# Keys of the second attention layer turned on VectorE, biases added on VectorE, sample products spread over three steps

## The reference, cut to what matters

```python
q, k, v = proj[..., :D], proj[..., D:2*D], proj[..., 2*D:3*D]
lf = log_sigmoid(proj[..., 3*D:] + b_f)
c = cumsum(lf, axis=1)                      # samples: over 256 cached and 16 new rows
s = einsum('bqhd,bkhd->bhqk', q, k) * 64 ** -0.5
s = s + cq[:, :, :, None] - ck[:, :, None, :]
s = where(kpos <= qpos, s, -inf)
o = einsum('bhqk,bkhd->bqhd', softmax(s), v)
y = o @ w_out
```

## Time and profile before

| | |
|---|---|
| median of 3 runs | 1886.15 us (1883.71 to 1886.22) |
| profiled execution, span | 1885.1 us (the page gives no time of its own beside the span) |
| TensorE busy | 1849.9 us (98%) |
| VectorE busy | 983.0 us (52%) |
| ScalarE busy | 722.0 us (38%) |
| GpSimd busy | 225.9 us (12%) |
| DMA | 259.38 MB, mean 138 GB/s |
| granted TensorE clock, mean | 0.997 |

### The profile page before, as it was taken

How to read it: one execution, slowest core, us unless ns; L and a number is a source line. 1 busy time by engine, 2 the same in 40 slices (tenths; PEclk the granted TensorE clock), 3 DMA queues, 4 the chain that set the end, 5 groups by cost and what they waited for, 6 DMA issues and landing times.

```text
span 1885.1 us, 29064 instructions
## 1 busy us (share of the span) xinstructions
PE 1849.9 (98%) x12004; PEld 1642.4 (87%) x12004; DVE 983.0 (52%) x1569; ACT 722.0 (38%) x1144; POOL 225.9 (12%) x357
## 2 busy tenths in 40 slices
PE   8999999999999999999999999999999999999998
PEld 8777799998888887799998899998897777999986
DVE  4557653443567778743443664443465576543434
ACT  4246443333255454333332343333242463433321
POOL 3114070000011222230000100000031230000000
PEclk9999999999999999999999999999999999999999
DMA  7357254433353433444433434433364562444332
GB/s 246 128 203 229 81 160 123 129 129 123 117 164 105 125 116 104 118 139 125 124 134 123 146 101 125 132 124 125 110 206 150 200 221 90 137 132 124 128 129 79
DMA packets 179171, 259.38 MB, mean 138 GB/s; under 512 B 14717, under 2 KB 122349, under 8 KB 179040
## 3 DMA queue, kind: packets, MB, share of 16 engines
q1 hardware_dynamic: 161184, 197.18, 32.3%
q0 software_dynamic: 17856, 60.35, 9.9%
HBM read 243.19 MB, written 13.19 MB: 136 GB/s over the span
## 4 chain that ended last, share of the span: by engine, by line
PE 90%; DVE 4%; ACT 3%; issue 1%; DMA 1%; SPq 0%; DVEq 0%; ACTq 0%
PE ps L1605 14%; PE ps L1607 14%; PE ps L1606 14%; PE ps L1617 11%; PE ps L1615 11%; PE ps L1616 11%; PE ps L1833 1%; PE ps L1951 1%; PE ps L1938 1%; PE ps L1638 1%; PE ps L1888 1%; PE ps L1671 1%; DVE w_lo L785 1%; PE ps L1908 1%; PE ps L1673 1%
## 5 line engine op out<-in xcount | busy, mean ns | idle before, releaser
L785 DVE TENSOR_TENSOR w_lo<-w_raw,w_hi 128x1024 fp32r<-128x1024 f32 x370 | 452.1, 1228 | 709.1 <-ACT w_hi L439 707.9
L439 ACT ACTIVATE w_hi<-w_raw 128x1024 fp32r<-128x1024 f32 x370 | 389.3, 1059 | 803.5 <-DMA w_raw<-in_w_ffn_in_dram 363.1
L1605 PE MATMUL ps<-xT_hi,w_hi 128*128 128x384 f32 x1568 | 528.4, 337 | 2.5 <-issue 1.4
L1607 PE MATMUL ps<-xT_hi,w_lo 128*128 128x384 f32 x1568 | 527.0, 336 | 0.0
L1606 PE MATMUL ps<-xT_lo,w_hi 128*128 128x384 f32 x1568 | 526.9, 336 | 0.0
L1605 PEld LDWEIGHTS ps<-xT_hi,w_hi 128*128 128x128 f32 x1568 | 294.8, 188 | 5.2 <-issue 5.1
L1606 PEld LDWEIGHTS ps<-xT_lo,w_hi 128*128 128x128 f32 x1568 | 294.8, 188 | 0.1
L1607 PEld LDWEIGHTS ps<-xT_hi,w_lo 128*128 128x128 f32 x1568 | 294.8, 188 | 0.0
L1617 PE MATMUL ps<-w_hi,hT_lo 128*128 128x512 f32 x528 | 210.6, 399 | 0.0
L1616 PE MATMUL ps<-w_lo,hT_hi 128*128 128x512 f32 x528 | 208.1, 394 | 0.0
L1615 PE MATMUL ps<-w_hi,hT_hi 128*128 128x512 f32 x528 | 207.4, 393 | 0.0
(11 more groups left out here) (329 smaller groups left out, 2021.8 us busy)
## 6 DMA issues: line engine op xcount, KB each, us to landing
w_raw<-in_w_ffn_in_dram SPq DMA_DIRECT2D x352, 256.0 KB, 3.2
w_raw<-in_w_ffn_out_dram SPq DMA_DIRECT2D x176, 256.0 KB, 2.9
w_raw<-in_w_fox_in_dram SPq DMA_DIRECT2D x96, 256.0 KB, 2.9
k_c<-in_cache_fox_k_dram POOLq DMA_DIRECT2D x32, 512.0 KB, 5.3
v_c<-in_cache_fox_v_dram POOLq DMA_DIRECT2D x32, 512.0 KB, 4.0
w_raw<-in_w_hgrn_in_dram SPq DMA_DIRECT2D x64, 256.0 KB, 2.9
w_raw<-in_w_fox_out_dram SPq DMA_DIRECT2D x32, 256.0 KB, 2.9
out_dram<-kv_tok POOLq DMA_DIRECT2D x4, 1024.0 KB, 5.0
```

The lines of the kernel that those rows point to most:

```text
L439: nc.scalar.activation(w_hi[:, slot, :], w_raw[:, slot, :], ACT.Copy).then_inc(hi_ready, 1)
L785: V.tensor_tensor(w_lo[:, slot, :], w_raw[:, slot, :], w_hi[:, slot, :].bitcast(F32), ALU.subtract).then_inc(lo_ready, 1)
L1605: mm(out, w_hi[:, slot, cols], x_hi[:, k, :], start=k == 0, stop=False, skip_group_check=True)
L1607: last = mm(out, w_lo[:, slot, cols], x_hi[:, k, :], start=False, stop=k == KD - 1, skip_group_check=True)
```

## The change

1. Biases and masks of the scores leave TensorE. SyncE writes the running sums to DRAM (`sums_p`, `sums_s`) and reads them back as broadcasts over partitions (`bias_p` for two prompt heads, `bias_s` for one sample), two buffers each, one broadcast after each step, each issued after the one before has landed (`next_bias`). GpSimd adds the mask in place (`mask_prompt_bias`, `mask_sample_bias`). Queries are scaled by -1/8, the sums keep their sign, and VectorE's tensor_tensor_reduce adds bias to scores, writes the sum to SBUF and takes its minimum; exp then reads SBUF with scale -1. The splits, selectors and the mask copies for TensorE go.
2. In layer 3 (`AHEAD`) cached keys are not turned in the loop. In the feed-forward of layer 2 GpSimd loads them in eight parts (`k_nat`), VectorE transposes them in blocks of 32x32 (8 instructions a part), GpSimd stores them to DRAM as `keys_t`, and SyncE loads them in layer 3, turned, in three buffers. GpSimd copies the new keys beside them.
3. In layer 3 the sample products of one step are spread over three (`steps_apart`): scores of n, transposes of n-1, s_out of n-2, fold of n-3. In layer 0 the order within a step changes: s_fold stands between other products, and s_keys is halved around s_turn.

```diff
+            def first_biases(i, j):
+                f = FOX[i]
+                sync.wait_ge(*at(f["c"], 1 + DB))
+                sync.dma_start(sums_p[j, :, 0:P], cp[:, 0:P]).then_inc(f["bias_in"][0], 16)
+                sync.dma_start(sums_p[j, :, P:T], cp[:, :]).then_inc(f["bias_in"][0], 16)
+                for hf in range(2):
+                    sync.dma_start(sums_s[j, :, :, hf, :], craw[8 * hf:8 * hf + 8, :, :]).then_inc(f["bias_in"][0], 16)
+                sync.wait_ge(*at(f["bias_in"], LOADED))
+                for k in range(2):
+                    prompt_bias_in(i, j, k)
+                for b in range(2):
+                    sample_bias_in(i, j, b)
+            def prompt_bias_in(i, j, k):
+                sync.dma_start(bias_p[:, k % 2, :, :], sums_p[j, 2 * k:2 * k + 2, :].partition_broadcast(P)).then_inc(
+                    FOX[i]["bias_in"][0], 16)
+            def sample_bias_in(i, j, b):
+                sync.dma_start(bias_s[:, b % 2, :, :],
+                               sums_s[j, :, b, :, :].rearrange("h f k -> h (f k)").unsqueeze(1).broadcast_to(
+                                   [HEADS // 2, DT, 2 * (PAST + DT)])).then_inc(FOX[i]["bias_in"][0], 16)
+            def next_bias(i, j, t):
+                f = FOX[i]
+                sync.wait_ge(*at(f["bias_in"], LOADED + 16 * (3 + t)))
+                if t % 2:
+                    sync.wait_ge(*at(f["nmax"], t + 1))
+                    prompt_bias_in(i, j, t // 2 + 2)
+                else:
+                    sync.wait_ge(*at(f["s_nmax"], t))
+                    sample_bias_in(i, j, t // 2 + 1)
+            def turned_keys(i, first, end):
+                ...
+                    else:
+                        sync.wait_ge(*at(f["s_scores"], n - KV + 1))
+                    sync.dma_start(k_t[:, n % KV, :, 0:PAST], keys_t[b, hf * WCOLS:(hf + 1) * WCOLS, :].rearrange(
+                        "(g p) k -> p g k", p=P)).then_inc(KEYS[f"in{n % KV}"][0], 16)
...
-                    chunks(w_fox_in[j], s["mix"], 6, 0 if i else 1)
-                    chunks(w_fox_out[j], s["out"], 2)
+                    if i == AHEAD:
+                        chunks(w_fox_in[j], s["mix"], 6, 0, 5 * CU)
+                        turned_keys(i, 0, KV)
+                        chunks(w_fox_in[j], s["mix"], 6, 5 * CU)
+                    else:
+                        chunks(w_fox_in[j], s["mix"], 6, 1)
+                    first_biases(i, j)
+                    chunks(w_fox_out[j], s["out"], 2, 0, RING)
+                    for t in range(1, 2 * DB - 2):
+                        if i == AHEAD:
+                            turned_keys(i, t + KV - 1, t + KV)
+                        if t < 2 * DB - 3:
+                            next_bias(i, j, t)
+                    chunks(w_fox_out[j], s["out"], 2, RING)
...
+            def turn_keys_ahead(n):                        # VectorE, in the feed-forward of layer 2, chunks 1 to 8
+                dve.wait_ge(*at(KEYS["loaded"], 16 * (n + 1)))
+                if n:
+                    dve.wait_ge(*at(KEYS["stored"], 64 * n))
+                for a in range(TWIN):
+                    ins = V.transpose(k_turn[:, :, :, a], k_nat[:, a, :])
+                ins.then_inc(KEYS["turned"][0], 1)
...
-                        V.tensor_reduce(nmx[:, (n - 1) % 2, 2:3], ps[:, SS_BANK, 0:PAST + DT], AX_X, ALU.max,
-                                        negate=True).then_inc(f["s_nmax"][0], 1)
+                        if n % 2:
+                            dve.wait_ge(*at(f["bias"], sample_bias(n // 2)))
+                        V.tensor_tensor_reduce(out=p_s[:, (n - 1) % 2, :], in0=ps[:, SS_BANK, 0:PAST + DT],
+                                               in1=bias_s[:, (n - 1) // 2 % 2, (n - 1) % 2, :], scale=1.0, scalar=LARGEST, op0=ALU.add,
+                                               op1=ALU.min, accum_out=nmx[:, (n - 1) % 2, 2:3]).then_inc(f["s_nmax"][0], 1)
...
+                        if n % 2 == 0:
+                            dve.wait_ge(*at(f["bias"], prompt_bias(n // 2)))
+                        for q, lo, hi in ((0, 0, P), (1, P, T)):
+                            ins = V.tensor_tensor_reduce(out=p_p[:, n % 2, lo:hi], in0=ps[:, bank, lo:hi],
+                                                         in1=bias_p[:, n // 2 % 2, n % 2, lo:hi], scale=1.0, scalar=LARGEST, op0=ALU.add,
+                                                         op1=ALU.min, accum_out=nmx[:, n % 2, q:q + 1])
...
+                def mask_prompt_bias(k):                   # GpSimd
+                    blocks = bias_p[:, k % 2, :, :].rearrange("p e (t c) -> p e t c", t=NTOK)[:, :, 0:NTOK:2, :]
+                    G.tensor_tensor(blocks, blocks, causal[:, :].unsqueeze(1).unsqueeze(1).broadcast_to([P, 2, 2, P]),
+                                    ALU.subtract).then_inc(f["bias"][0], 1)
+                def mask_sample_bias(b):
+                    new = bias_s[:, b % 2, :, PAST:]
+                    G.tensor_tensor(new, new, new_mask[:, :].unsqueeze(1).broadcast_to([P, 2, DT]), ALU.subtract).then_inc(
+                        f["bias"][0], 1)
...
                 for n in range(KV, 2 * DB + KV):
-                    if n < 2 * DB:
+                    if n < 2 * DB and i == AHEAD:
+                        pool.wait_ge(*at(f["s_scores"], n - KV + 1))
+                        new_keys(n)
+                    elif n < 2 * DB:
                         pool.wait_ge(*at(f["ktr"], n - KV + 1))
                         load_k(n)
+                    if i == AHEAD and 2 <= n - KV < 2 * DB - 2:
+                        next_mask(n - KV)
                     pool.wait_ge(*at(f["s_o"], n - KV + 1))
                     if n < 2 * DB:
                         load_v(n)
                     if n - KV + 2 < 2 * DB:
                         load_new(n - KV + 2)
+                    if i != AHEAD and 2 <= n - KV < 2 * DB - 2:
+                        next_mask(n - KV)
...
-                        mm(out, sel_p[:, h:h + 1].broadcast_to([CROWS, P]), c_p[:, :], start=True, stop=False, skip_group_check=True)
-                        mm(out.rearrange("p (t c) -> p t c", t=NTOK)[:, 0:NTOK:2, :], ident_r[:, :],
-                           causal_r[:, :].rearrange("p (t c) -> p t c", t=NTOK)[:, 0:NTOK:2, :], start=False, stop=False,
-                           skip_group_check=True)
...
-                    mm(ps[:, SS_BANK, 0:PAST + DT], sel_s[:, n % 2, :], c_s[:, n // 2, :], start=False, stop=True,
-                       skip_group_check=True).then_inc(f["s_scores"][0], 1)
...
+                def steps_apart():                         # layer 3; layer 0 keeps a loop like the one before
+                    for n in range(HEADS):
+                        if n >= 3 and n % 2:
+                            p_out((n - 3) // 2)
+                        if n % 2 == 0:
+                            p_scores(n // 2)
+                        ...
+                        if n >= 2:
+                            s_out(n - 2)
+                        if n:
+                            s_turn(n - 1)
+                            p_turn(n - 1)
+                        s_pairs(n)
+                    s_fold(HEADS - 3)
+                    out_piece(0, 0)
+                    s_turn(HEADS - 1)
+                    p_turn(HEADS - 1)
+                    out_piece(0, 1)
+                    s_out(HEADS - 2)
+                    p_out(KD - 1)
+                    out_piece(1, 0)
+                    s_fold(HEADS - 2)
+                    s_out(HEADS - 1)
+                    out_piece(1, 1)
+                    s_fold(HEADS - 1)
```

377 lines of the change are left out of this document (226 added, 151 removed).

## The result

The changed kernel takes 1924.29 us (median of 4 runs, 1918.36 to 1928.68) against 1885.05 us of the kernel before on the same chip: a ratio of 1.0207, 95% interval 1.0191 to 1.0223. It is slower by some 39 us. The forecast was 1876, the range ended at 1892.

The account below looks back on a forecast made before the run. TensorE, busy 98% of the span, was taken as the bound, with DMA deciding in L3's changed loop. L0 -4.2, L3 -6.8 and +1.0 ahead of the loops gave -10.0: 1885.1 to 1875.1, forecast 1876 us, range 1858 to 1892.

Parts of the forecast that it names:

- Removed products: Attention loops: bias, causal and key-transpose products leave TensorE, 9.9 us in L0 and 23.8 in L3, if TensorE stayed the limit.
- Added DMA: Attention loops: broadcasts and other transfers need 63.4 us of fully used DMA in L0, 64.0 in L3; loops 72.7 and 73.4.
- rival B: Loops: SyncE issues each bias only after the last landed, so a landing bounds the step; about +13, 1899 us; chance 0.13.
- DMA allows a gain of 5.3 and 4.6: DMA's limit on the two attention loops against 78.0 us: 5.3 us less in L0, 4.6 less in L3.
- Added waits in L0: L0's loop: VectorE and TensorE wait for late GpSimd masks, leaving L0 a gain of 4.2 us.
- rival D: L0's loop: GpSimd's mask and VectorE's scaling of probabilities exclude each other in SBUF; +4 to +8 us, 1882; chance 0.05.
- New operation on VectorE: Head loops: tensor_tensor_reduce takes as long as the reduce it replaces, nothing added; exp from SBUF within 0.1 us.
- Ahead of the loops: Before both loops: output weights land some 4 us later behind the biases; 0.5 us a layer, +1.0 in all.
- Keys in the third feed-forward: Third feed-forward: 64 VectorE transposes, up to 0.67 us each, and added DMA are covered; nothing, bounds 0 to 2 us.

Follow-up runs that it names:

- e4: Changed kernel without the broadcasts inside the loops and their masks, first biases added again, computation partly left out: 1887.83 us, ratio 1.0010.
- e3: Changed kernel with prompt and sample bias broadcasts counted on two semaphores, so two can be under way: 1913.75 us, ratio 1.0146.
- e10: Changed kernel without broadcasts inside the loops, but with all GpSimd masks, laid again on the first biases: 1896.27 us, ratio 1.0056.
- e8: Kernel before plus only turned keys and spread sample products, with the new order inside a step; biases stay on TensorE: 1886.66 us, ratio 1.0010.
- e5: The changed kernel run again unaltered, as the measure for runs beside it: 1923.74 us, ratio 1.0206.
- e15: Keys' part alone, biases on TensorE, order inside a step as before, turning blocks behind chunks 1 to 8: 1877.85 us, ratio 0.9961.
- e12: Keys' part alone, biases on TensorE, order as before, turning blocks behind chunks 1, 2, 4, 5, 7, 8, 9, 10: 1875.19 us, ratio 0.9953.
- e2: Changed kernel with layer 3's keys again transposed by TensorE in its loop, so only the biases' part, new order in both loops: 1915.85 us, ratio 1.0155.

## Why the prediction was wrong

**Removed products: right in the main.** With no broadcasts and masks (e4) loop 0 is 4.9 us shorter and loop 3 13.0; without what the new order costs (below) it would be 8.6 and 18.7, beside 9.9 and 23.8 of removed products. After its waits the text had booked 4.2 and 6.8.

**Added DMA: the step that failed.** The bytes and rates were right: the DMA engines' busy time in the loops is 0.76 x 85.8 = 65.2 us and 0.77 x 84.2 = 64.9, forecast 63.4 and 64.0. Wrong was the next line, a share of 0.95 outside 6 unused us, from which a shorter loop followed. Measured: a share of 0.88 and 0.89 over the 72.5 and 71.0 us in which transfers run, and 13 us around them with almost none, so 72.5 + 13.3 in place of 66.7 + 6 in loop 0. And as the engines fill, everything lands later, which the text has only under its rival B. The loads of v, in the first loop before, the two loops of the changed kernel, and the second of e3:

```profile
v_c<-in_cache_fox_v_dram POOLq DMA_DIRECT2D x13, 512.0 KB, 4.0
v_c<-in_cache_fox_v_dram POOLq DMA_DIRECT2D x13, 512.0 KB, 5.5
v_c<-in_cache_fox_v_dram POOLq DMA_DIRECT2D x13, 512.0 KB, 6.7
v_c<-in_cache_fox_v_dram POOLq DMA_DIRECT2D x13, 512.0 KB, 7.2
```

A high share alone does not hold TensorE. In the second loop of e4, without broadcasts, the DMA engines have 0.96 over 40 us and TensorE works through:

```profile
1505.00:1545.00 40.00, 38.39 (x518) 23.33 (x516) 26.20 (x135) 26.27 (x102) 15.29 (x31) 1.00 0.96 320
```

That the three buffers per operand and the waits across queues keep the changed loops from using the engines so well is argued; no run has more buffers. The Trainium skill, "DMA: Bandwidth & Descriptors", section "Where 436 GB/s comes from", has some 358 GB/s for one core. Over 40 us the runs stay below it, 298 in e3 (share 0.98) and 320 in e4; over the ten us from 4 to 14 of the changed kernel they move 388, so it is no bound for a short stretch. The forecast of "DMA allows a gain of 5.3 and 4.6" should have been a loss: +6.2 and +4.7 measured.

**Rival B: named, only a part.** Its cadence came true: from the third on, the broadcasts inside the loops go out 5.3 and 5.2 us apart (156.8 to 204.1 and 1534.5 to 1581.0), where it decides from 5.2 on. But by its own sum that gives only about 1887 (79.4 and 75.2 us against 76.2 each, less 2.2, plus 1), and even 5.7 gives 1899. (The range was said to take in B up to 5.5; by the same sum 5.5 is 1894, outside it.) With the chain gone (e3) the loops keep most of their loss: of 11 to 13 us it explains 3.5 to 4.8 by the stages. The medians give it up to 11 of the 39. It got 0.13.

**Added waits in L0: right in kind, a little small, and with another reason in it.** Masks alone cost 7.5 us in e10; the text had 9.9 less 4.2, 5.7. It had them as waits for a late mask, and VectorE does wait 7.8 us for sample masks in e10. Beside that stands the lock of rival D, which had a chance of 0.05: the scalings take 9.2 us longer. How the 7.5 us divide is not shown; D's price of 4 to 8 us on top of the 5.7 was too high, its mechanism is real.

**A step that is missing: the order.** The text costed what was removed and never the fold moved into the middle of the score and value products, or the keys' transposes cut in two. Under the limit of TensorE that is 3.6 us in loop 0 and 5.7 in loop 3.

**New operation on VectorE: right.** The sum with minimum takes 442 ns for 128x272 (e4), as long as the reduction it replaces (0.44 in the earlier trace rows), and 0.08 us for reading the accumulator. ScalarE's exp of these takes 522 ns from SBUF (e4) against 487 from PSUM (before), within the 0.1 us allowed.

**Ahead of the loops: mis-sized.** +0.5 each became +5.5 and +8.0. The text had a landing some 4 us later and took little of it to reach TensorE. SyncE issued 3.9 and 6.5 us later, the first square then shared the engines with 1.34 MB of broadcasts and landed 6.7 us after its issue (2.8 before), and the copies of turned keys stood behind it in ScalarE's queue. Waits in the changed kernel between 100 and 136 us, and ScalarE's in e8 (100 to 128):

```profile
ACT w_hi L527 <- DMA w_raw<-in_w_fox_out_dram: 15.6, 2, 9.9
PE ps L1991 <- ACT kT L664: 5.7, 1, 5.7
...
ACT w_hi L488 <- DMA w_raw<-in_w_fox_out_dram: 7.8, 4, 3.5
```

**Keys in the third feed-forward: mis-sized.** 0 with bounds 0 to 2 became some 4 (283.6 to 288.0, 1 to 5 over the thirteen profiles). A block needs 4.5 us of transposes, then 2.3 in which GpSimd issues four stores, and then the next load, which lands 11 us after its issue: 18 in all, in chunks of 16.6, so VectorE waited at the head of its queue for six of the eight blocks. 64 transposes took 0.735 us each, above the bound of 0.67.

**The start** (+2.3) is not shown to be the change's: the profiles with the change, whole or in part, lie between 45.1 and 49.0, and there is one of the kernel before (45.8). In the changed kernel's profile the first products of 384 columns run at the lower clock level, 0.32 us apart, until 16.8 us; in e5, the same kernel, at the upper from the first on.

## What to carry to other kernels

Before a product is traded for a transfer, ask what share the DMA engines have in the part of the stage in which transfers can run: here the mean of 0.62 hid 0.71 in the middle, and a quarter more bytes took that to 0.88, with every load landing later and the loops longer than before. Bytes that would fit the time can still cost more than the products that they replace. A change of several parts is to be costed and tried part by part: here the keys' part alone, with the old order, is 0.4% (e15) to 0.5% (e12) faster than the kernel before, and the biases' part with the new order (e2) 1.6% slower. And price a moved instruction too, not only the added and removed ones.
